# A hybrid decoder step on one core: sample state products four at a time, and up products as three single passes

## The reference

```python
num = w_prev[..., None] * jnp.einsum('bhtd,bhde->bhte', q_c, C) + jnp.einsum('bhts,bhse->bhte', wts, v_c)
...
C = wp[..., None, None] * C + jnp.einsum('bhs,bhsd,bhse->bhde', ws, k_c, v_c)
```

## Time and profile before

| | |
|---|---|
| median of 3 runs | 1915.89 us (1915.38 to 1916.56) |
| the profiled execution | 1918.07 us, its span 1916.1 us |
| mean granted TensorE clock | 0.96 of full speed |
| TensorE busy | 1748.7 us, 91% |
| VectorE, ACT, POOL busy | 910.2, 604.8 and 270.5 us |
| L1084, the up products | 73.5 us (o_ml) and 73.3 us (o_pool) busy |

### The profile page before, as it was taken

The page is one execution under the profiler, slowest core; times in us unless marked ns, Lnnn a source line. Parts: engine busy times, 40 slices in busy tenths (PEclk is TensorE's granted clock), DMA queues, the critical chain, the costliest instruction groups (busy, mean ns, idle before and its releaser), DMA issues. The chain is left out here.

```text
span 1916.1 us, 36779 instructions
## 1 busy us (share of the span) xinstructions
PE 1748.7 (91%) x14891; PEld 1439.4 (75%) x14891; DVE 910.2 (48%) x1610; ACT 604.8 (32%) x890; POOL 270.5 (14%) x286
## 2 busy tenths in 40 slices
PE   7999999999999999999998999999898868777675
PEld 7999899998787778778777999999796434443242
DVE  6553445555756676576665445455423222121223
ACT  5243223333443344344335333335432101110012
POOL 0550003112010100100010000850050000000002
PEclk9999999999999999999998999999998988898888
DMA  7445353434232223233215446455638999999995
GB/s 270 174 155 187 110 179 117 173 135 167 100 112 90 99 101 122 87 112 112 90 55 204 155 175 250 152 220 214 238 159 338 422 431 432 431 431 431 431 431 248
DMA packets 46600, 408.98 MB, mean 213 GB/s; under 512 B 6580, under 2 KB 8376, under 8 KB 16696
## 3 DMA queue, kind: packets, MB, share of 16 engines
q1 hardware_dynamic: 46520, 407.81, 54.2%
HBM read 396.62 MB, written 11.18 MB: 213 GB/s over the span
## 5 line engine op out<-in xcount | busy, mean ns | idle before, releaser
L387 PE MATMUL ps<-x_high,w_high 128*128 128x288 f32 x928 | 257.4, 303 | 9.3 <-ACT w_high L593 9.3
L388 PE MATMUL ps<-x_rest,w_high 128*128 128x288 f32 x928 | 253.1, 299 | 0.0
L387 PEld LDWEIGHTS ps<-x_high,w_high 128*128 128x128 f32 x928 | 177.1, 191 | 12.8 <-ACT w_high L593 10.2
L388 PEld LDWEIGHTS ps<-x_rest,w_high 128*128 128x128 f32 x928 | 177.1, 191 | 0.5
L549 ACT ACTIVATE w_high<-w_raw 128x2048 fp32r<-128x2048 f32 x57 | 109.2, 1915 | 153.9 <-DMA w_raw<-in_w_main 77.5
L1101 PE MATMUL ps<-x_high,r_high 128*128 128x288 f32 x512 | 145.8, 308 | 3.8 <-ACT r_high L1352 3.8
L660 DVE TENSOR_TENSOR w_rest<-w_raw,w_high 128x2048 fp32r<-128x2048 f32 x58 | 137.1, 2369 | 11.0 <-ACT w_high L549 11.0
L2557 PE MATMUL ps<-half_a,xg 128*32 128x512 f32 x240 | 81.4, 840 | 62.3 <-DMA half_b<-in_w_egu 62.0
L1101 PE MATMUL ps<-rx_low,r_high 128*128 128x288 f32 x480 | 134.7, 305 | 0.0
L392 PE MATMUL ps<-x_high,w_rest 128*128 128x288 f32 x928 | 132.1, 295 | 1.0 <-DVE w_rest L660 1.0
L392 PEld LDWEIGHTS ps<-x_high,w_rest 128*128 128x128 f32 x928 | 126.0, 188 | 1.2 <-DVE w_rest L660 1.2
(11 more groups left out here) (600 smaller groups left out, 3824.1 us busy)
## 6 DMA issues: line engine op xcount, KB each, us to landing
w_raw<-in_w_main SPq DMA_DIRECT2D x57, 1024.0 KB, 4.8
ring<-in_w_g SPq DMA_DIRECT2D x32, 1024.0 KB, 4.8
half_a<-in_w_egu SPq DMA_DIRECT2D x15, 2048.0 KB, 18.0
half_b<-in_w_egu SPq DMA_DIRECT2D x15, 2048.0 KB, 22.3
ring<-in_w_u SPq DMA_DIRECT2D x32, 512.0 KB, 4.2
ring<-in_w_gate SPq DMA_DIRECT2D x8, 2048.0 KB, 7.8
ring<-in_w_out SPq DMA_DIRECT2D x8, 2048.0 KB, 7.8
half_d<-in_w_egu SPq DMA_DIRECT2D x8, 2048.0 KB, 20.7
```

Of the source, the lines that this page charges most:

```text
L387: mm(o, high[:, t % 2, k, :], x_h[:, k, :], start=(k == 0), stop=False)
L388: ins = mm(o, high[:, t % 2, k, :], x_l[:, k, :], start=False, stop=False)
```

## The change

In the input stage:
- The 8 sequences are taken as two rounds of four (`QUADS` = 4). The state products of `numerators` go to four different groups of 32 PSUM rows; the four partial sums are put together by the identity product that was there before, over 128 rows now. The sample values, keys and gates are written four times, on 128 partitions, by small products with the identity. `ktm` holds for each group of 32 partitions the keys of two sequences (128 x 256 elements, 32 x 1024 before). `decode_state` is one step with all eight products, each reading 32 partitions of its own and writing one of four banks. `scores` of the next head waits for the states' last half, `numerators` did before.
- ACT writes high halves of the pool outcome (a second scaled copy) and of the mLSTM outcome (`outcome_high`), POOL the low halves (`o_l`, `outcome_rest`), the latter in place over `o_ml` and `o_pool`.
- At the end ACT makes the high half of the first up weight and POOL its low half.

In the recurrent stage:
- An up product is 24 single passes: 16 with the weight's high half (`up_h`, one buffer for all products), on the outcome's high and low halves in turn, then 8 with its low half (`up_rest`, in place over the loaded weight). ACT makes `up_h` (steps j00 to j11), POOL `up_rest` (r00 to r11). The next `up_h` waits for the 16 passes of the product before (steps V00 to V11) and for POOL's subtraction.
- The fillers are dealt out anew, and the second half of ACT's split of G11 comes later (step i11), where j11 stands instead; VectorE's second half of that low part comes after s0.
- ACT's and POOL's loops run seven times and the eighth turn is written out, without j00 and r00.

```diff
@@ numerators, decode_state
-                    ins = mm(ps[0:NSM, 0, 0:DV], qz[:, NSM * b:NSM * b + NSM], cst[:, h % 2, b, :], start=(b == 0), stop=(b == NB - 1))
+                    ins = mm(ps[quad(b % QUADS), 0, 0:DV], qz[:, NSM * b:NSM * b + NSM], cst[:, h % 2, b, :],
+                             start=(b < QUADS), stop=(b >= NB - QUADS))
...
+                for b in range(NB):
+                    n, m = b % QUADS, b // QUADS
+                    ins = mm(ps[:, state_banks[n], m * DV:(m + 1) * DV], ktm[quad(n), m, :], vt[quad(n), 2, h * DV:(h + 1) * DV],
+                             start=True, stop=True)
@@ turn_values (the same for the keys and the gates)
+                            for n in range(QUADS):
+                                ins = mm(o[quad(n), :], own[:, NPR:T], ident, start=True, stop=True)
@@ filler, an up product
                         for t in range(lo, hi):
-                            src = (o_ml, o_pool)[b]
-                            ins = mm(ps[:, (1, 7)[b], 0:T], w_up[:, b, t, :], src[:, t, :], start=(t == 0), stop=(t == KH - 1))
+                            k = t // 2 if t < 2 * KH else t - 2 * KH
+                            if t < 2 * KH:
+                                ins = mm(o, up_h[:, k, :], (o_h, o_l)[t % 2][:, KH * b + k, :], start=(t == 0), stop=False)
+                                if t == 2 * KH - 1:
+                                    q.done(ins, "V" + name[1:])
+                                continue
+                            if k == 0:
+                                pe.wait_ge(g_.sem, g_.at("r" + name[1:], of))
+                            ins = mm(o, up_rest[:, b, k, :], o_h[:, KH * b + k, :], start=False, stop=(k == KH - 1))
@@ the order of the fillers (passes of a product, from:to)
-                filler("U00", 0, 8)
-                filler("U01", 0, 4)
+                filler("U00", 0, 24)
+                filler("U01", 0, 20)
...
-                filler("U01", 4, 8)
+                filler("U01", 20, 24)
...
-                filler("G10", 22, 32)
+                filler("G10", 22, 31)
                 forward(2)
-                filler("U10", 0, 2)
+                filler("U10", 0, 7)
                 back(2)
...
-                filler("U10", 2, 4)
+                filler("U10", 7, 14)
                 forward(3)
-                filler("U10", 4, 6)
+                filler("U10", 14, 16)
+                filler("G10", 31, 36)
                 back(3)
...
-                filler("U10", 6, 8)
+                filler("G10", 36, 43)
                 forward(4)
-                filler("G10", 32, 40)
+                filler("G10", 43, 48)
+                filler("U10", 16, 18)
                 back(4)
...
-                filler("G10", 40, 48)
+                filler("U10", 18, 24)
...
-                filler("U11", 0, 2)
+                filler("U11", 0, 6)
@@ ACT, recurrent stage
+                def up(name, of):
+                    n = order.index(name)
+                    act.wait_ge(up_slots[n % 2], of * 32 + 16 * (n // 2) + 16)
+                    act.wait_ge(q.sem, q.at("V" + order[n - 1], i))
+                    act.wait_ge(g_.sem, g_.at("r" + order[n - 1], i - 1 if n == 1 else i))
+                    a.done(fn(up_h[:, :, :], w_up[:, n % 2, :, :], ACT.Copy), "j" + name)
...
+                up("01", i)
                 split("00")
...
                 split("10")
+                up("10", i)
...
                     if l == 4:
-                        split("11", 8, 16)
+                        up("11", i)
@@ POOL, recurrent stage
+                def rest(name):
+                    b = int(name[1])
+                    g_.done(tt(up_rest[:, b, :, :], w_up[:, b, :, :], up_h[:, :, :], ALU.subtract), "r" + name)
+                pool.wait_ge(a.sem, a.at("j01", i))
+                rest("01")
```

More of the change, by code:

```diff
@@ L1099, in filler @@
                         k = t // 2 if t < 2 * KD else t - 2 * KD
+                        if name == "G11" and t == KD:
+                            pe.wait_ge(a.sem, a.at("i11", i))
                         if t < 2 * KD:
@@ L1240, in _ @@
                 q.done(ins, "u5")
-                filler("U11", 2, 4)
+                filler("U11", 6, 12)
                 pe.wait_ge(a.sem, a.at("td", i))
@@ L1247, in _ @@
                 q.done(ins, "z6")
-                filler("U11", 4, 6)
+                filler("U11", 12, 18)
                 pe.wait_ge(a.sem, a.at("z6", i))
@@ L1253, in _ @@
                 q.done(ins, "u6")
-                filler("U11", 6, 8)
+                filler("U11", 18, 24)
                 vt = lambda c, h, n=P: tok[0:n, c, 64 * h:64 * h + 64]
@@ L1343, in _, with turn @@
             order = ["00", "01", "10", "11"]
-            with act.Fori(0, N) as i:
+            def turn(i, last=False):
                 def split(name, lo=0, hi=KD):
@@ L1430, in _ @@
                 a.done(fn(ek, ek, ACT.Sqrt), "groot")
+            with act.Fori(0, N - 1) as i:
+                turn(i)
+            turn(N - 1, last=True)
             act.wait_ge(q.sem, q.at("U11", N - 1))
@@ L1675, in _, with turn @@
                 nc.gpsimd.tensor_copy(low(k), x_old[:, k, :]).then_inc(xl_in, 1)
-            with pool.Fori(0, N) as i:
+            def turn(i, last=False):
                 level = lambda l, n: K("level_c")[:, l * BLK:(l + n) * BLK].rearrange("p (l t) -> p l t", l=n)
+                def rest(name):
[3 more added lines that the diff above has]
+                rest("01")
                 pool.wait_ge(v.sem, v.at("bc", i))
@@ L1692, in _ @@
                 pool.wait_ge(g_.sem, g_.at("sx1", i))
+                pool.wait_ge(a.sem, a.at("j10", i))
+                rest("10")
                 pool.wait_ge(v.sem, v.at("m01", i))
@@ L1695, in _ @@
                 g_.done(tt(m, m, gtmp[:, :], ALU.add), "m0")
+                pool.wait_ge(a.sem, a.at("j11", i))
+                rest("11")
                 pool.wait_ge(a.sem, a.at("sas", i))
                 g_.done(spread(vnx[:, :, :], tok[0:2 * NSM, 2, 0:P]), "nx")
+                if last:
+                    g_.left_out(pool, "r00", i)
+                else:
+                    pool.wait_ge(a.sem, a.at("j00", i))
+                    rest("00")
                 pool.wait_ge(v.sem, v.at("m11", i))
@@ L1700, in _ @@
                 g_.done(tt(m, m, gtmp[:, :], ALU.add), "m1")
+            with pool.Fori(0, N - 1) as i:
+                turn(i)
+            turn(N - 1, last=True)
             pool.wait_ge(q.sem, q.at("U11", N - 1))
```

168 lines of the change are left out of this document (105 added, 63 removed).

## The result

The changed kernel takes 1927.25 us (median of 8 runs, 1922.13 to 1940.27), the kernel before in the same comparison 1916.61 (8 runs). The ratio is 1.0053, 95% interval [1.0032, 1.0075]: slower by some 10 us, where I forecast 8.8 us less. 1927.25 lies outside my range too. The outcome is on rival 3's side. All ratios here leave out runs far above the rest of their kernel, which are two of the twelve of experiment 10 (2185 and 4175 us).

The account below looks back on a forecast made before the run. TensorE was taken to bound the input and recurrent stages, transfers the last 416 us. Input stage -18.4 and loop +9.6 gave -8.8 against the 1915.89 median: 1907.1 us, eight times in ten between 1893 and 1918.

Parts of the forecast that it names:

- rival 3: Recurrent stage: POOL's four subtractions per iteration hold VectorE where it is the limit; loss 2.9 us each, 1920.7 us; chance 0.13.
- input stage: State products and updates overlap in array quarters, saving 22.0 us, less 3.1 for four-fold transposes and gates: net -18.9 us.
- its end: End of input stage: ACT's copy of the first up weight and POOL's subtraction come behind the last tile, +0.5 us.
- loop: Eight iterations of the recurrent stage, each +0.7 at the top and +0.5 in the gaps: +9.6 us.
- Top of the iteration: U01 waits 1.6 us for ACT's copy behind a table load; L1116 1.9 late, +0.7 us remaining, bounds +0.2 to +1.5.
- held by POOL for about 1.2: Top of an iteration: POOL's subtraction delays VectorE's chain, which delivers G01's low half, by about 1.2 us, not 1.9.
- The gaps: Block inverse with fillers dealt out anew: waits, savings of two products and POOL's subtraction give +0.5 us, bounds -1.2 to +0.9.
- l10 wait: In the gap behind forward(3), TensorE waits 1.55 us at G10's pass 32 for VectorE's low half.
- z6 wait: Gap between u5 and z6: POOL's subtraction of U11's half beside VectorE's three copies, priced at +0.2 us.
- rival 1: Gaps of the block inverse are free, VectorE's l10 comes before TensorE; loop gives -2.4, time 1895.1 us; chance 0.19.
- rival 2: Everything the passes save arrives, -18.4 in the input stage and -20.8 in the loop: 1877 us; chance 0.03.
- rival 4: Input stage: quarters overlap only by half, sets of eight take 1.8 to 2.0 us; time 1914.1 us; chance 0.13.

Follow-up runs that it names:

- experiment 10: Kernel before with its input table of constants two columns wider in HBM alone, only the old columns loaded: 1918.74 us, ratio 1.0006.
- experiment 1: Kernel before with only the new state products, transposes and their waits in the input stage, up products and loop untouched: 1904.32 us, ratio 0.9927.
- experiment 3: Changed kernel without ACT's copy ahead of U01, which uses U00's high half, POOL making its low half early: 1918.38 us, ratio 1.0006.
- experiment 4: Changed kernel with each of POOL's up-weight subtractions made on one of eight blocks: 1918.0 us, ratio 0.9995.
- experiment 6: Changed kernel with U10 before G10's third pass in the gaps and U01 reusing U00's high half, POOL's subtractions whole: 1900.96 us, ratio 0.991.
- experiment 7: Kernel before with the new input stage alone, plus G10's third pass put before the third back step: 1915.74 us, ratio 0.9993.
- experiment 9: Kernel before with only the additional two-column table of constants, loaded and read by nothing: 1922.08 us, ratio 1.0021.

## Why the prediction was wrong

The balance in the prediction's own terms, for the profiled executions (+5.7 in the span; forecast -8.8):

| term | forecast | measured |
|---|---|---|
| input stage | -18.9 | -18.8 (experiment 1, against traces with the same clock) |
| its end | +0.5 | +1.4 (-17.5 from 473.6 to 456.14 for the first up product, against -18.8) |
| loop | +9.6 | +19.8 (2.4 from the first up product to the first z, 16.7, 0.7) |
| behind the loop | 0 | +3.3 |

**Input stage: right, and by the mechanism.** I took 1.06 us for each set of eight from L1178; they take 1.07 and 1.15. The Trainium skill (TensorE: Matmul & The Clock Gate, "Part 3: Packing small matmuls") with its 2.38, which is for three column tiles, and 3.07, for four row tiles, would as an estimate have had 1.5 and 1.3. Here it is 3.64 / 1.07 = 3.4 for four column groups and 3.98 / 1.15 = 3.5 for four row groups, and the measurement decides.

**The end of the input stage: mis-sized.** TensorE idles 4.0 us there, 2.7 before: the next stage begins when ACT's copy and POOL's subtraction behind the last tile are done (POOL ends at 455.31, the new stage's first instructions start at 455.68).

**Top of the iteration: the right step, too small.** The table load, the copy behind it, the 1.6 us wait and the late z came as worked out, 2.1 for 1.9. G01's third passes start 22.10 us after U00 (619.40 - 597.30). Before it was 20.95 (629.79 - 608.84): +1.15, where I had +0.7. What failed is the line "held by POOL for about 1.2": VectorE's row is held for 1.5 (2.02 for 0.52) in seven of eight turns. It starts inside POOL's 2.48 us and ends 0.3 after it; I had leaned on POOL starting in a gap of VectorE, and that is no matter of chance: ACT's written order, the last root and then the copy, fixes the place of both. Experiments 3 and 4 price this place and the other of POOL.

**The gaps: the failed step.** I had +0.5 with bounds to +0.9. Measured: g0, the first product behind them, starts 2.27 us later against U00 than before (54.26 for 51.99), that is +1.12 for the gaps. The l10 wait was forecast, even larger than it came. The z6 wait was not: I put 0.2 on POOL's subtraction beside VectorE's three copies, and it makes 0.8 to 1.0 (experiments 4 and 6), again because one instruction with two SBUF inputs, `dx`, falls into it in most iterations. And I counted the l10 wait against what the passes save, so the step looked nearly free; experiment 7 shows that the wait alone costs 1.4 us in each iteration.

**What the prediction had no term for.** The clock: of the three iterations with half clock two take 70.1 and one 69.5, in place of 69.4, in the profiled run, and the kernel's run-to-run spread of 18 us goes with the mean clock, from 0.956 at 1922.13 us to 0.944 at 1940.27. That this is the rest of the way from +5.7 in the span to +10.6 in the medians is likely, not shown: only one of the runs has a trace. The two traced kernels also differ by the length of the half clock at the first up product, 3.4 and 6.8 us. And the table: +3 us of the +3.3, by experiments 9 and 10.

**The rivals.** Rival 3 had the sign, the price per iteration (2.3 needed, 2.5 measured) and, with 1920.7, a time too low by 6.5. But its cause, POOL alone, isn't what decided: taking POOL out leaves the kernel at 0.9995, taking out the order of the gaps gives 0.9981, and only the three together give 0.9856. Rivals 1 and 2 are refuted by the 1.24 and the 1.58 us waits, rival 4 by the 1.07 and 1.15 us. The forecast was wrong because three small prices of one iteration went up together, one inside its bounds, one past them, and one (the clock) without any.

## What to carry to other kernels

A pass saved on TensorE is worth something only where its operands come no later: list for each new split the engine's order in front of it (here a table load) and each two-input instruction on VectorE that POOL's new work will meet, and price the meeting with the whole rest of POOL's instruction, since written-out orders meet in the same place every time. Convert the products whose splits fit idle places (here two of four, 1895 us) and leave the others. With none of the up products changed the time is 1904 us, with all four 1927. A wait put into a stretch of sparse small products costs its own length and may cost the clock behind it. Compare the rate of the transfers before and after a change too, when it moves the layout of SBUF.

## What the runs showed of the hardware

- POOL's subtraction of 1024 columns takes 2.36 to 2.48 us, not the 1.89 of a 64-partition product, and a VectorE instruction with two SBUF inputs that starts inside it ends about 0.3 us after it (0.52 becomes 2.02, 0.47 becomes 1.40). The Trainium skill (GPSIMD Engine Reference, "1. Specifications") says that GpSimd contends with VectorE instructions of two SBUF inputs; the trace agrees and gives the size.
- TensorE's granted clock fell to half behind idle times of 1.1 to 1.3 us among sparse small products, in 12 of 32 iterations, for 3.4 us in most and up to 10.2 in some (experiments 3 and 4), with TensorE busy while it lasted. It fell as well near 197 us behind idle times of 0.55 and 0.76 us, in 6 of 14 traces, and not behind 1.58 us between dense passes.
- Eight more bytes on each partition of a table that nothing reads took the transfers of the expert stage from 431 to 428 GB/s, 3 us. A table that was longer in HBM alone left 432.
